# Last stage of a decoder layer: three token tiles' residual stored to the output early, ScalarE scaling their gated rows, GpSimd adding them by an accumulating transfer

## The reference, cut to what matters

```python
h = modulate(rms_norm(x, g_pre_mlp[l]), sh2, sc2)
y = jnp.square(jax.nn.relu(h @ w_ff1[l])) @ w_ff2[l]
x = x + gt2[:, None, :] * rms_norm(y, g_post_mlp[l])
```

## Time and profile before

| what | value |
|---|---|
| median of 3 runs | 2170.28 us (2169.17 to 2170.95) |
| profiled execution, its own time | 2170.66 us |
| profiled execution, span | 2168.9 us |
| TensorE (PE) busy | 2107.8 us, 97% of the span |
| VectorE (DVE) busy | 1614.6 us, 74% |
| ScalarE (ACT) busy | 797.7 us, 37% |
| GpSimd (POOL) busy | 99.5 us, 5% |
| read from and written to HBM | 313.20 MB, 10.52 MB |

### The profile page before, as it was taken

How to read it: one execution, slowest core, us unless ns; L and a number is a source line. 1 busy time by engine, 2 the same in 40 slices (tenths; PEclk the granted TensorE clock), 3 DMA queues, 4 the chain that set the end, 5 groups by cost and what they waited for, 6 DMA issues and landing times.

```text
span 2168.9 us, 25152 instructions
## 1 busy us (share of the span) xinstructions
PE 2107.8 (97%) x9025; PEld 1678.0 (77%) x9025; DVE 1614.6 (74%) x1863; ACT 797.7 (37%) x1035; POOL 99.5 (5%) x105
## 2 busy tenths in 40 slices
PE   5999999999999999999999999999999999999997
PEld 4777778778778777878778778778778787787785
DVE  7998597875977887686686776776866767767766
ACT  5324612224552265243343343343332433433433
POOL 1001050000220001000000000000000000000000
PEclk8999999999999999999999999999999999999999
DMA  9995458845437763322332332333323323323333
GB/s 331 364 288 173 137 185 293 294 162 191 136 131 254 272 215 99 99 96 87 118 100 91 106 97 87 106 98 105 97 95 109 97 87 107 98 92 117 98 122 150
DMA packets 181582, 324.57 MB, mean 150 GB/s; under 512 B 12648, under 2 KB 49624, under 8 KB 179216
## 3 DMA queue, kind: packets, MB, share of 16 engines
q1 hardware_dynamic: 173600, 302.08, 43.1%
q0 software_dynamic: 3568, 16.95, 2.1%
q10 hardware_dynamic: 4352, 4.73, 0.7%
HBM read 313.20 MB, written 10.52 MB: 149 GB/s over the span
## 4 chain that ended last, share of the span: by engine, by line
PE 68%; DVE 16%; issue 7%; ACT 5%; DMA 2%; SPq 1%; DVEq 0%; ACTq 0%
PE pair L834 9%; PE pair L836 9%; PE pair L835 9%; PE pair L859 7%; PE pair L860 7%; PE pair L861 7%; PE bank L526 4%; PE bank L527 4%; PE bank L528 4%; PE bank L536 2%; PE bank L538 2%; PE bank L537 2%; DVE acc L1442 2%; ACT w_hi L1263 2%; DVE w_lo L1414 2%
## 5 line engine op out<-in xcount | busy, mean ns | idle before, releaser
L1862 DVE TENSOR_TENSOR yg<-yg,pair 128x1024 f32<-128x1024 f32 x240 | 289.8, 1218 | 315.6 <-PE pair L861 315.6
L834 PE MATMUL pair<-h_hi,w_lo 128*128 128x512 f32 x1020 | 404.6, 397 | 0.0
L836 PE MATMUL pair<-h_hi,w_hi 128*128 128x512 f32 x1020 | 403.9, 396 | 0.0
L835 PE MATMUL pair<-h_lo,w_hi 128*128 128x512 f32 x1020 | 403.5, 396 | 0.0
L859 PE MATMUL pair<-w_hi,op_lo 128*128 128x512 f32 x840 | 333.4, 397 | 2.3 <-DVE op_lo L1829 2.2
L860 PE MATMUL pair<-w_lo,op_hi 128*128 128x512 f32 x840 | 332.8, 396 | 0.0
L861 PE MATMUL pair<-w_hi,op_hi 128*128 128x512 f32 x840 | 331.9, 395 | 0.0
L964 ACT ACTIVATE w_hi<-raw 128x1024 fp32r<-128x1024 f32 (+1 forms) x114 | 118.7, 1044 | 324.1 <-DMA raw<-in_w_in_dram 201.3
L836 PEld LDWEIGHTS pair<-h_hi,w_hi 128*128 128x128 f32 x1020 | 191.9, 188 | 46.8
L835 PEld LDWEIGHTS pair<-h_lo,w_hi 128*128 128x128 f32 x1020 | 192.0, 188 | 46.4 <-issue 0.2
L834 PEld LDWEIGHTS pair<-h_hi,w_lo 128*128 128x128 f32 x1020 | 191.7, 188 | 46.5 <-issue 0.2
(11 more groups left out here) (272 smaller groups left out, 2781.0 us busy)
## 6 DMA issues: line engine op xcount, KB each, us to landing
raw<-in_w_ada_dram SPq DMA_DIRECT2D x128, 512.0 KB, 4.6
w_raw<-in_w_ff_dram SPq DMA_DIRECT2D x128, 512.0 KB, 3.8
raw<-in_w_ff_dram SPq DMA_DIRECT2D x128, 512.0 KB, 4.5
raw<-in_w_in_dram SPq DMA_DIRECT2D x74, 512.0 KB, 4.7
gst<-in_w_ada_dram SPq DMA_DIRECT2D x64, 512.0 KB, 9.5
raw<-in_w_out_dram SPq DMA_DIRECT2D x32, 512.0 KB, 4.8
x_tok<-in_x_dram SPq DMA_DIRECT2D x4, 1024.0 KB, 8.4
xr<-in_x_dram POOLq DMA_DIRECT2D x4, 1024.0 KB, 7.7
```

Of the source, the lines that this page charges most:

```text
L834: pe.matmul(b, lo[:, cols], h_hi[:, kt, :], start=(kt == 0), stop=False)
L835: pe.matmul(b, hi[:, cols], h_lo[:, kt, :], start=False, stop=False)
L836: last = pe.matmul(b, hi[:, cols], h_hi[:, kt, :], start=False, stop=(kt == KT - 1))
L1862: dve.tensor_tensor(y, y, pairs[2 + (i + r) % 2][:, :, :], ALU.subtract if i == 6 else ALU.add).then_inc(product_read, 1)
```

## The change

`BY_SUM = 3`: tiles 0, 1 and 2 no longer go through `finish`. Their `x1` is stored straight to the output tensor in the middle of the program, in place of the scratch tensor, and isn't loaded back. ScalarE multiplies their gated rows by `rstd` into `x1r` (`scale_out`, two ACTIVATE of 1024 columns for each tile), and GpSimd adds the 1 MB tile to the output by one accumulating transfer. Tile 3 is computed and stored as before. `fin_sum` now also counts the reciprocals.

```diff
-            for t in range(NT):
+            for t in range(BY_SUM, NT):
                 for part in range(2):
-                    sp.wait_ge(out_ready, 2 * t + part + 1)
+                    sp.wait_ge(out_ready, 2 * (t - BY_SUM) + part + 1)
...
+            def scale_out(t):
+                act.wait_ge(fin_sum, 2 * t + 2)
+                act.wait_ge(y2_gated, 8 + 2 * t + 2)
+                for part in range(2):
+                    src = (tile_cols(y2, t, 0), gated[:, t % 2])[part]
+                    act.activation(tile_cols(x1r, t, part), src, ACT.Copy,
+                                   scale=stat[:, FR + t:FR + t + 1]).then_inc(out_scaled, 1)
+
             for t in range(NT):
                 for r in range(2):
                     act.wait_ge(y2_done, 4 + 2 * t + r + 1)
                     act.wait_ge(f_ssq, 8 + 2 * t + r)
                     act.activation(junk3[:, 0, :], rest(t, r), ACT.Square,
                                    accum_out=stat[:, FS + 4 * t + 2 + r:FS + 4 * t + 3 + r]).then_inc(f_ssq, 1)
-                act.wait_ge(fin_sum, t + 1)
+                    if t and not r:
+                        scale_out(t - 1)
+                act.wait_ge(fin_sum, 2 * t + 1)
...
             def scale_known(t):
                 dve.wait_ge(fin_std, t + 1)
-                step(dve.reciprocal(stat[:, FR + t:FR + t + 1], stat[:, FR + t:FR + t + 1]))
-                dve.wait_ge(x1r_in, 16 * NT)
+                dve.reciprocal(stat[:, FR + t:FR + t + 1], stat[:, FR + t:FR + t + 1]).then_inc(fin_sum, 1)
...
             for t in range(NT):
+                if t >= 2:
+                    dve.wait_ge(out_scaled, 2 * (t - 1))
                 close_rest(t, 0)
                 if t:
                     scale_known(t - 1)
-                    finish(t - 1, 0)
-                    finish(t - 1, 1)
                 close_rest(t, 1)
                 dve.wait_ge(f_ssq, 8 + 2 * t + 2)
                 dve.tensor_reduce(stat[:, FR + t:FR + t + 1], stat[:, FS + 4 * t:FS + 4 * t + 4], AX, ALU.add).then_inc(fin_sum, 1)
             scale_known(NT - 1)
-            finish(NT - 1, 0)
-            finish(NT - 1, 1)
+            dve.wait_ge(fin_sum, 2 * NT)
+            dve.wait_ge(x1r_in, 16 * (NT - BY_SUM))
+            for t in range(BY_SUM, NT):
+                finish(t, 0)
+                finish(t, 1)
...
-                pool.dma_start(x1_scr[t * P:(t + 1) * P, :], yg[:, t, :]).then_inc(x1_stored, 16)
+                pool.dma_start((out2 if t < BY_SUM else x1_scr)[t * P:(t + 1) * P, :], yg[:, t, :]).then_inc(x1_stored, 16)
...
-            for t in range(NT):
+            for t in range(BY_SUM, NT):
                 pool.dma_start(x1r[:, t, :], x1_scr[t * P:(t + 1) * P, :]).then_inc(x1r_in, 16)
+            for t in range(BY_SUM):
+                pool.wait_ge(out_scaled, 2 * (t + 1))
+                pool.dma_start(out2[t * P:(t + 1) * P, :], x1r[:, t, :], accum_op=ALU.add).then_inc(x1_stored, 16)
+            pool.wait_ge(x1_stored, 16 * (NT + BY_SUM))
```

More of the change, by code:

```diff
@@ L112, in hybrid_layer @@
     LAST_COLS = (0, 2, 1, 3)
+    BY_SUM = 3
     SUMS_AT = {14: 0, 20: 1, 26: 2, 28: 3, 33: 4, 36: 5, 40: 6, 45: 7, 52: 8, 57: 9}
@@ L291, in hybrid_layer @@
         f_ssq, y2_gated, fin_std, out_ready, stored = (sem(n) for n in ("f_ssq", "y2_gated", "fin_std", "out_ready", "stored"))
+        out_scaled = sem("out_scaled")
         XS, XR, RL, RA, YS, YR, X1S, X1R_, FS, FR, NM, ES, X1H = 0, 4, 8, 12, 16, 32, 40, 44, 48, 64, 72, 80, 84
@@ L503, in _ @@
                 load_w2((LAST, 0), 1, which)
-            for t in range(NT):
+            for t in range(BY_SUM, NT):
                 for part in range(2):
-                    sp.wait_ge(out_ready, 2 * t + part + 1)
+                    sp.wait_ge(out_ready, 2 * (t - BY_SUM) + part + 1)
                     dst = out2[t * P:(t + 1) * P, :].rearrange("p (s r c) -> p s r c", s=2, r=2)[:, :, part, :]
                     sp.dma_start(dst, tile_cols(x1r, t, part)).then_inc(stored, 16)
-            sp.wait_ge(stored, 16 * 2 * NT)
+            sp.wait_ge(stored, 16 * 2 * (NT - BY_SUM))
         @block.tensor
```

## The result

The changed kernel takes 2174.57 us (median of 12 runs, 2171.59 to 2178.68) against 2169.04 us before (12 runs, 2165.51 to 2171.56). The ratio is 1.0025, with a 95% interval of 1.0018 to 1.0033: slower by 5.5 us, or 0.25%. The prediction was 2170.9 us, which is 0.6 above the kernel before, with a range to 2177.5; the case "slower by over 0.2%" had a chance of 0.21. It came true, though the interval begins just under 0.2%.

The account below looks back on a forecast made before the run. It took VectorE to bound the last stage before, and the DMA queue after: 2150.6 + 3 times 5.1 + 2.7 + 0.9 gives a span of 2169.5, 0.6 later than before, so 2170.9 us against the median; range 2167.2 to 2177.5.

Parts of the forecast that it names:

- slower by over 0.2%: Outcome case: the accumulating add costs more than its bytes, x from 6.33 on, over 4.3 us slower; chance 0.21.
- a dear add: Rival for the accumulating transfers: three passes or a rate below plain ones; x 7.6 gives 2178.4 us; chance 0.21.
- x: Time one 1 MB accumulating transfer fills the DMA engines: taken as 5.1 us, bounds 2.5 and 7.6.
- two reads: Forecast's own case: each accumulating transfer reads SBUF and HBM, x 4.4 to 6.3, time 2168.9 to 2174.6; chance 0.47.
- the prediction's sum: Span end from the full DMA queue: 2150.6 + 3x + 2.7 + 0.9 = 2154.2 + 3x, or 2169.5.
- The beat: Last stage, one tile's sum to the next: 4.46 us instead of 5.46, three beats giving back 3.0 us.
- the new wait of VectorE: VectorE's wait on `out_scaled` in front of tiles 2 and 3: claimed to cost nothing.
- The fewer loads: Three 1 MB loads less between 2106 and 2122: ScalarE's 6.63 us weight wait shrinks, costed at nothing for the end.
- The term 3x: Part of the span's end: three accumulating transfers one after the other in one full DMA queue, x being 5.1 us.
- about 6.6 for the first, 7.5 for the second: Sign: landing times in us of the accumulating transfers behind their issues, more for the third.
- The queue: DMA engines at the end: one full queue from 2150.6 on, three transfers, then the last tile's two stores of 2.7 us.
- 0.9 to the end, whichever comes last: End of the span: 0.9 us from the last data moved, whichever transfer comes last.

Follow-up runs that it names:

- e5: Changed kernel with the add left out of GpSimd's transfers and SP, not GpSimd, waiting for them at the end: 2167.68 us, ratio 0.9991.
- e1: Changed kernel with the add left out, so GpSimd's three transfers are plain stores: 2167.25 us, ratio 0.9988.
- e10: Changed kernel with only tiles 0 and 1 by whole-tile accumulating transfers (BY_SUM = 2), SP waiting at the end: 2169.42 us, ratio 1.0006.
- e9: e6 with tile 0's residual added from the scratch tensor into the scaled rows in SBUF, SP storing the tile afterwards: 2170.84 us, measured once.
- e6: Changed kernel with only tile 0 by accumulating transfer (BY_SUM = 1), SP waiting at the end: 2169.01 us, ratio 0.9996.
- e7: e4 with accumulating transfers for halves of tiles 0 and 1 only (BY_SUM = 2), VectorE finishing tile 2 whole: 2167.66 us, ratio 0.9988.
- e3: Kernel before, with one added wait of GpSimd at its end for SP's eight stores: 2174.99 us, ratio 1.0024.
- e2: Changed kernel with SP instead of GpSimd waiting at the end for the accumulating transfers: 2171.89 us, ratio 1.0012.
- e4: e2 with tiles 0 to 2 split: VectorE finishes part 0, ScalarE scales part 1 for a 512 KB accumulating transfer: 2167.66 us, ratio 0.9994.
- e8: e4 without accumulating transfers: all residuals loaded, GpSimd adds part 1 of tiles 0 to 2 by tensor_tensor, SP stores: 2170.72 us, ratio 1.0005.

## Why the prediction was right, and where not

The range held the time. The step from the kernel before was forecast as 0.6 us and measured as 5.5, so the likeliest number was some 5 us too low as a step (3.7 us in the time itself, since the kernel before took 1.2 us less in all twelve runs than in the first three). That the time still lies in the range is in part luck. The upper part of the range stood for a dear add, x up to about 7.3, and the case "slower by over 0.2%" asked for x from 6.33 on. The add cost 5.5, inside the forecast's own case "two reads". With that x the prediction's sum gives 2154.2 + 3 x 5.5 = 2170.6, which is 1.7 us later than before. The rest came from the end of the span, for which the range had no room of its own. Point by point:

- **The beat.** Right: 4.42 to 4.44 us measured, 4.46 forecast, ScalarE's pair in the middle of it, the new wait of VectorE without a price, 3.08 us gained for 3.0. e5 shows 2.7 of them in the end of the span.
- **The fewer loads.** Right as to the wait: ScalarE's copy no longer waited for a DMA, and it waited for PE instead. That nothing was won ahead of the mark is not shown, since the mark moves by more from run to run.
- **x, the price of an accumulating transfer.** 5.5 us against the 5.1 taken. It was bounded from 2.5 to 7.6 and set by two reads for one write. e1 measured the lower end, 2.5. The term 3x was thus 1.1 us too small. The Trainium skill, in "Collectives: The Full Stack", section "Part 3: Why 7× under link rate — side-by-side accounting", says of the reduce step of a collective that its two sources go through one read ring and halve the rate. The 205 against 410 GB/s in full engines (e10) and e9 agree with that. That the read side is the cause is not shown by them: an adder at that pace would look the same. The sign "about 6.6 for the first, 7.5 for the second" missed: they landed 8.0 and 9.7 us behind their issues.
- **The queue.** Right in kind: the engines were full from 2154 to 2173, and e10, e6 and e7 followed the number of transfers. The flow began 0.4 us later than taken (2154.0, 17.9 behind the mark, against 17.45). The issue comes 0.3 us behind the pair's end, and the data begin 1.3 us behind the issue instead of 1.05.
- **The end of the span.** Here a step failed: "0.9 to the end, whichever comes last". It took the tail of SP's stores in the kernel before for every transfer and every engine. Behind GpSimd's last wait come 4.15 us of drain. In the changed kernel this costs 2.0 us over SP's own end (2176.9 against about 2174.9), the largest single term of the miss, and in the kernel before it costs 4.2 us when a wait alone is added (e3). SP's tail was longer too: its end is 1.9 us behind 2173, where the full engines end, and not 0.9. The drain's row was in the trace of before, hidden 43 us ahead of the end; it showed that a drain outlasts GpSimd's last landing, by 2.0 us, and not that it is 4.15 us when it starts late.

From the mark to the end, 36.35 was forecast (2169.5 less 2133.15) and 40.78 measured. Of the 4.4 us between them 1.1 come from x, 0.4 from the later start of the flow, 1.0 from SP's tail and 2.0 from the drain, which is the whole within the rounding. Why SP's tail is 1.0 us longer stays open. Against the kernel before, the queue took back the 3.1 us that the engines had gained and 2.1 more; the tail and the drain make the rest of the 5.0.

## What to carry to other kernels

At the end of a program each engine has an end of its own: here it paid to let SP wait for the last transfers (e1 to e5, e2 to the changed kernel). Look at the drain rows at the end of the program before a wait or a transfer is given to GpSimd there. A transfer that adds took 2.2 times the DMA engines' time of a plain store here (5.5 us against 2.5 for 1 MB), so price it against what else they carry in the next microseconds. The only version with the add whose interval lies below the kernel before is the one that gave it to halves of the first two tiles (e7); with two whole tiles (e10) nothing was gained. Where a beat of two engines is shortened, ask which queue then sets the end, since the last stage's gain is worth only what the slowest of engines, queues and drains lets through.

## What the runs showed of the hardware

- GpSimd's drain at the end of its program takes 4.147 us when it begins behind its last wait with nothing of GpSimd's pending (after, e1, e3). When it begins earlier, it ends 2.0 to 2.3 us behind the last landing of GpSimd's transfers (before, e2, e4 to e7, e9, e10; for example e6: 2158.6 behind 2156.55), and 4.2 us behind the last add of GpSimd where that comes last (e8: 2166.55 behind 2162.36). The drains of VectorE, ScalarE and TensorE end with their engine's last instruction (after: VectorE's 2.5 us end at 2165.1, as its last `finish` does), and SP's takes 7 ns.
- An accumulating transfer of 1 MB fills the engines for 5.5 to 5.8 us and lands 7.8 to 8.0 us behind its issue when none is ahead of it, with the sum in HBM (e6) or in SBUF (e9); three in a row landed after 8.0, 9.7 and 10.8 us. A plain one takes 2.5 us and lands after 4.1 to 4.2 (e1). With runs of 2 KB an accumulating one takes 3.5 us for 512 KB (e4), where a plain store of SP in such runs takes 1.3 (before: 2.7 for two).
- Stores of SP that meet it are held up: 512 KB landed in 8.8 to 9.3 us in the changed kernel, against 3.1 to 3.7 before.
- A tensor_tensor of VectorE with both inputs in SBUF took 2.20 to 2.27 us instead of 0.69 beside GpSimd's (e8).
